# A hybrid decoder block in fp32r: operand tiles moved to other SBUF offsets, three copies moved between ScalarE and VectorE, and one step of the decay sums brought forward

## The reference, cut to what matters

```python
h = rms_norm(x, norm_pre_w)
proj = h @ w_in                                  # 10256 columns
qkv_a, z_a, beta_a, dec_a, qkv_b, z_b, gate_logits = split(proj)   # beta_a, dec_a: 8 columns each
qkv_a = silu(causal_depthwise_conv(qkv_a, conv_w))
beta = sigmoid(beta_a)
g = -exp(dn_a_log) * softplus(dec_a + dn_dt_bias)
oa = gated_delta_rule(qa, ka, va, g, beta)       # uses running sums of g and exp of their differences
ya = rms_norm(oa, dn_onorm_w) * silu(z_a)
ob = causal softmax attention(qb, kb, vb) with a relative-position bias
yb = ob * silu(z_b)
gates = sigmoid(gate_logits + b_gate)
merged = gates[0] * (ya @ w_branch[0]) + gates[1] * (yb @ w_branch[1])
out = x + rms_norm(merged @ w_out, norm_post_w)
```

## Time and profile before

| what | value |
|---|---|
| median of three runs | 364.14 us |
| profiled execution, its own time | 364.33 us |
| its span in the trace | 362.5 us |
| granted TensorE clock | 0.998 of full |
| TensorE busy (matmul) | 352.6 us, 97% |
| VectorE, ScalarE, GpSimd busy | 74%, 61%, 16% |
| DMA, mean rate | 172 GB/s |

### The profile page before, as it was taken

The page is one execution under the profiler, slowest core; times in us unless marked ns, Lnnn a source line. Parts: engine busy times, 40 slices in busy tenths (PEclk is TensorE's granted clock), DMA queues, the critical chain, the costliest instruction groups (busy, mean ns, idle before and its releaser), DMA issues.

```text
span 362.5 us, 7455 instructions
## 1 busy us (share of the span) xinstructions
PE 352.6 (97%) x2755; PEld 337.1 (93%) x2755; DVE 267.5 (74%) x559; ACT 222.3 (61%) x500; POOL 59.5 (16%) x113
## 2 busy tenths in 40 slices
PE   7999999999999999999999999999999999999893
PEld 5889997999999999999999999999999999998682
DVE  2869777488986868979787897878976656576744
ACT  4778895545466576686767677677685645334431
POOL 1533434400052000301103030030301000000011
PEclk9999999999999999999999999999999999999999
DMA  8667848896699484456645564475447557583533
GB/s 264 171 189 190 278 122 229 205 289 174 172 254 213 121 223 123 118 133 169 166 118 146 153 168 118 121 202 143 118 121 199 147 152 196 142 266 116 203 146 116
DMA packets 100305, 62.48 MB, mean 172 GB/s; under 512 B 4676, under 2 KB 95214, under 8 KB 100270
## 3 DMA queue, kind: packets, MB, share of 16 engines
q1 hardware_dynamic: 98014, 58.59, 59.1%
q0 software_dynamic: 1072, 3.04, 2.8%
q10 hardware_dynamic: 1184, 0.39, 0.5%
HBM read 60.41 MB, written 1.59 MB: 171 GB/s over the span
## 4 chain that ended last, share of the span: by engine, by line
PE 88%; DVE 4%; ACT 3%; DMA 1%; issue 1%; POOL 0%; DVEq 0%; SPq 0%; ACTq 0%; POOLq 0%
PE banks L1321 62%; PE banks L1339 6%; PE banks L1534 5%; ACT w_hi L637 3%; DVE w_lo L887 2%; DMA xin<-in_x_dram 1%; PE banks L1419 1%; PE banks L1396 1%; DVE th_E L1169 1%; PE banks L1436 1%; PE banks L1425 1%; PE banks L1306 1%; DVE th_a L1165 1%; PE banks L1238 1%; PE banks L1385 1%
## 5 line engine op out<-in xcount | busy, mean ns | idle before, releaser
L887 DVE TENSOR_TENSOR w_lo<-raw,w_hi 128x1024 fp32r<-128x1024 f32 x102 | 123.9, 1218 | 54.3 <-ACT w_hi L637 51.3
L637 ACT CAST w_hi<-raw 128x1024 fp32r<-128x1024 f32 x103 | 107.2, 1045 | 8.4 <-DMA raw<-in_w_out_dram 3.5
L1321 PE MATMUL banks<-h_hi,w_hi 128*128 128x256 f32 x568 | 82.1, 286 | 0.0
L1321 PE MATMUL banks<-h_lo,w_hi 128*128 128x256 f32 x568 | 78.0, 279 | 0.0
L1321 PE MATMUL banks<-h_hi,w_lo 128*128 128x256 f32 x568 | 77.8, 279 | 0.0
L1321 PEld LDWEIGHTS banks<-h_hi,w_hi 128*128 128x128 f32 x568 | 71.4, 188 | 0.3
L1321 PEld LDWEIGHTS banks<-h_hi,w_lo 128*128 128x128 f32 x568 | 71.2, 188 | 0.0
L1321 PEld LDWEIGHTS banks<-h_lo,w_hi 128*128 128x128 f32 x568 | 71.2, 188 | 0.0
L961 DVE SCALAR_TENSOR_TENSOR acc<-banks,vec,acc 128x255 f32<-128x255 f32 (+2 forms) x72 | 34.5, 479 | 4.3 <-ACT acc L758 2.2
L587 POOL TENSOR_TENSOR so<-so,rnq 128x2 f32<-128x2 f32 x8 | 2.6, 329 | 164.9 <-ACT junk L825 164.9
L758 ACT ACTIVATE acc<-banks,vec 128x256 f32<-128x256 f32 x16 | 7.6, 473 | 19.2 <-PE banks L1321 19.2
(11 more groups left out here) (243 smaller groups left out, 545.5 us busy)
## 6 DMA issues: line engine op xcount, KB each, us to landing
raw<-in_w_in_dram SPq DMA_DIRECT2D x80, 512.0 KB, 5.2
raw<-in_w_branch_dram SPq DMA_DIRECT2D x16, 512.0 KB, 4.9
raw<-in_w_out_dram SPq DMA_DIRECT2D x8, 512.0 KB, 3.7
xin<-in_x_dram SPq DMA_DIRECT2D x2, 512.0 KB, 4.0
th_E<-g_rows POOLq DMA_DIRECT2D x2, 512.0 KB, 7.0
bias<-bias_rows POOLq DMA_DIRECT2D x1, 1024.0 KB, 7.6
raw<-in_x_dram SPq DMA_DIRECT2D x2, 512.0 KB, 5.7
out_dram<-xin SPq DMA_DIRECT2D x4, 256.0 KB, 2.0
```

Source lines behind the costliest of these rows:

```text
L637: nc.scalar.copy(w_hi[:, t % SLOTS, :], raw[:, t % SLOTS, :]).then_inc(s_hi, 1)
L887: v.tensor_tensor(w_lo[:, t % SLOTS, cols], raw[:, t % SLOTS, cols], w_hi[:, t % SLOTS, cols].bitcast(F32), ALU.subtract).then_inc(s_lo, 1)
L1321: last = mm(ps, w, r, start=part == 0 and k == 0, stop=part == 2 and k == KT - 1)
```

## The change

The order of the allocations changes, and three pieces of work move:
- `gt` (768 bytes of a partition), `wbd2` (1024), `ssqk` (64) and `ng` (64) are declared ahead of `raw`: 1920 bytes in all. `h_hi`, `h_lo`, `y_hi` and `y_lo` are declared behind `w_lo`. By the sizes, `raw`, `w_hi`, `w_lo`, `h_hi`, `h_lo`, `y_hi`, `y_lo`, `xin` and `cst` then start at multiples of 2 KB. `acc` and what follows it keep their offset past a multiple of 2 KB (576 for `acc`, `kT_all`, `act`, `bT`).
- The copy to `bd_T` at S = 5 goes from VectorE to ScalarE.
- The copies of the first half of `vtok_all` at S = 33 and 34 go from ScalarE to VectorE.
- VectorE's last step of g (L941 to L947) goes from S = 9 to S = 8, ahead of that step's `split_lo`.

```diff
+        gt = sb("gt", [P, 12, NC, HEADS])
+        wbd2 = sb("wbd2", [P, KT, 4 * HEADS], F32R)
+        ssqk = sb("ssqk", [P, NC, HEADS])
+        ng = sb("ng", [P, NC, HEADS])
         raw = sb("raw", [P, SLOTS, D])
         w_hi = sb("w_hi", [P, SLOTS, D], F32R)
         w_lo = sb("w_lo", [P, SLOTS, D], F32R)
+        h_hi = sb("h_hi", [P, KT, SEQ], F32R)
+        h_lo = sb("h_lo", [P, KT, SEQ], F32R)
+        y_hi = sb("y_hi", [P, 2, HEADS, SEQ], F32R)
+        y_lo = sb("y_lo", [P, 2, HEADS, SEQ], F32R)
         xin = sb("xin", [P, NC, D])
...
-        wbd2 = sb("wbd2", [P, KT, 4 * HEADS], F32R)
...
-        h_hi = sb("h_hi", [P, KT, SEQ], F32R)
-        h_lo = sb("h_lo", [P, KT, SEQ], F32R)
...
-        gt = sb("gt", [P, 12, NC, HEADS])
...
-        ng = sb("ng", [P, NC, HEADS])
...
-        ssqk = sb("ssqk", [P, NC, HEADS])
...
-        y_hi = sb("y_hi", [P, 2, HEADS, SEQ], F32R)
-        y_lo = sb("y_lo", [P, 2, HEADS, SEQ], F32R)
```

On ScalarE:

```diff
-                if S == 7:
+                if S == 5:
+                    sa.wait_ge(s_bd_m, 1)
+                    nc.scalar.copy(bd_T, bA[0:4 * HEADS, 0:SEQ]).then_inc(s_bd_t, 1)
+                elif S == 7:
...
-            def value_front(i):
-                group, c = i // NC, i % NC
+            def value_front(c):
                 if c == 0:
-                    sa.wait_ge(s_vg_p, group + 1)
+                    sa.wait_ge(s_vg_p, 2)
                 else:
-                    sa.wait_ge(s_tile, V_TILES[4 * group + 3] + 1)
-                nc.scalar.copy(vtok_all[:, c, 512 * group:512 * group + 512],
-                               ((bE, bF), (bB, bE))[group][c]).then_inc(s_vtok, 1)
+                    sa.wait_ge(s_tile, V_TILES[7] + 1)
+                nc.scalar.copy(vtok_all[:, c, 512:], (bB, bE)[c]).then_inc(s_vtok, 1)
```

On VectorE (`value_front` is called behind `similarity`, at S = 33 and 34):

```diff
-                if S == 5:
-                    ve.wait_ge(s_bd_m, 1)
-                    v.tensor_copy(bd_T, bA[0:4 * HEADS, 0:SEQ]).then_inc(s_bd_t, 1)
-                elif S == 7:
+                if S == 7:
...
-                elif S == 9:
+                elif S == 8:
                     ve.wait_ge(s_ga, 5)
                     ve.wait_ge(s_gs, 7)
...
+            def value_front(c):
+                if c == 0:
+                    ve.wait_ge(s_vg_p, 1)
+                else:
+                    ve.wait_ge(s_tile, V_TILES[3] + 1)
+                v.tensor_copy(vtok_all[:, c, 0:512], (bE, bF)[c]).then_inc(s_vtok, 1)
```

More of the change, by code:

```diff
@@ L844, in _ @@
                     decay(2 * (S - E0) + 1)
[L845 to L848, removed]
+                done = 3 * V_TILES[7] + 3
+                if S in (done, done + 1):
+                    value_front(S - done)
                 for g in range(HEADS):
@@ L1183, in _ @@
                     similarity(SIM[S])
+                done = 3 * V_TILES[3] + 3
+                if S in (done, done + 1):
+                    value_front(S - done)
                 for g in range(HEADS):
```

## The result

The changed kernel takes 368.75 us (median of four runs, 368.60 to 368.83) beside 364.22 us for the kernel before in the same comparison: ratio 1.0114, 95% interval 1.0088 to 1.0141. Its profiled execution took 368.75 us, with a span of 367.0 us, 4.5 us more than before's 362.5.

The account below looks back on a forecast made before the run. TensorE's own matmul pace was taken to bound most of the kernel, except the loop near the end. Value copies gave -0.22 us and the other three parts 0: 364.14 - 0.22 = 363.9 us, range 355.0 to 366.4.

Parts of the forecast that it names:

- Part 1, value copies: Value copies moved to VectorE end TensorE's wait at L1385 in key head 7; gain 0.20 to 0.25 us.
- Parts 2 and 3: The bd_T copy on ScalarE and the last step of g at S = 8: each taken as 0.
- Part 4, addresses: New start offsets of the tensors leave the matmul pace unchanged: taken as 0, ends -15 us and +2.2 us.
- for no effect: Argument for 0 from addresses: moving operands at different offsets past 2 KB, with stationary offsets differing as much, keep one pace.
- The prediction's own sign of being wrong: The prediction is wrong if the pace of the stream of 384 matmuls, 45.2 us, moves at all.
- The half-sentence *against: Counterpoint to no address effect: no moving operand or weight tile starts at a multiple of 256 bytes, so that grid was untried.
- The rule cited from the Trainium skill: TensorE waits for nobody at SBUF; only VectorE and GpSimd contend, so the address gain is 0.
- The estimate from "DMA: Bandwidth & Descriptors": First load of xin, 4.68 us: a start off a 256-byte boundary costs an extra transaction, estimated 0.28 us.
- The loop near the end: From 311.52 to 336.17 us VectorE and ScalarE bound seven rounds of 3.52 us; faster matmuls win nothing there.
- Rival three: The 22 fast tiles of the heads turn slow, 0.10 us each: +2.2 us, 366.1 us with part 1; chance 0.12.
- Rivals one and two: One: all tiles fast, stream 43.7 us, 356.8 us, chance 0.16. Two: no loss at all, 348.4 us, chance 0.10.
- the last chance, 0.05: Chance given to another wait or a pace slower than now: 0.05.

Follow-up runs that it names:

- the empty one: Block left out but for copying its input; groups of 48 fp32r matmuls with nothing else running: 120.0 ns a matmul at distance 0, 117.8 at 64.
- the 32-byte one: Changed kernel with h and y 32 bytes further than w instead of 0: 364.39 us, ratio 1.0001 to the kernel before.

## Why the prediction was wrong

**Part 1, value copies: right.** The timeline of VectorE with the moves alone (L991 is the new copy, L971 before's L974):

```profile
49.82 1.27 DVE L991 COPY vtok_all<-banks 128x512 f32<-128x512 f32 x2
51.33 1.23 DVE L887 TENSOR_TENSOR w_lo<-raw,w_hi 128x1024 fp32r<-128x1024 f32 x1 [0.23 <-ACT w_hi L637]
...
55.94 0.42 DVE L971 SCALAR_TENSOR_TENSOR kT_all<-tacc,acc 128x256 f32<-128x256 f32 x1
```

The execution is 0.44 us ahead of before's since the load of xin (4.24 us for 4.68 at the same address). The two copies take 1.27 us (predicted 1.36), the next `w_lo` begins at 51.33, 51.77 by before's clock (predicted 51.75), and the last step of key head 7 begins at 55.94, 56.38 by before's clock (57.35 before, 56.6 predicted). L1385's wait for L974 is gone; in the weight load's waits of the changed kernel nothing stands where it stood:

```profile
PEld banks L1278 <- issue: 0.4, 1, 0.4
```

The value stream begins 0.68 us earlier than before, 0.44 of it the load, so the part is worth 0.24 us. The medians give 0.44 (363.70 to 364.14); what the 0.2 beyond come from no run settles, and the ratio's interval, 0.9951 to 1.0000, is wider than that.

**Parts 2 and 3: right at 0.** L1278 keeps its 0.4 us at the issue, and no chain piece before 60 us is shorter or longer with the moves alone but by the wait above.

**Part 4, addresses: the step that failed, at the value 0 taken for it.** The argument *for no effect* was that moving operands at 1984, 704 and 128 all ran at one pace. But it looked at each operand's own start. What counts is the start of one less that of the other, and for h and y before's were the same in this measure: 1984 - 128 = 1856 = 7 x 256 + 64, and 704 - 128 = 576 = 2 x 256 + 64. The third, w at 128 past h at 1984, is 192 modulo 256, and a matmul of 512 columns, so it was no second sample. "Stationary offsets differ as much" was false modulo 256: every slice of `w_hi` and `w_lo` starts 128 past a multiple of 256. What I read as independent offsets was one distance, so its evenness could say nothing about another. The new layout puts the distance at 0, the slowest of the multiples of 16 bytes measured: 120.0 ns for 117.8. The term taken as 0 measured 5.05 us (363.70 to 368.75): in the ledger 0.84 on the long stream and 4.4 on the tiles behind it, with 0.37 won back in the output. The prediction's own sign of being wrong, that the stream's pace moves at all, came true. The half-sentence *against* (no start at a multiple of 256 was ever tried) asked for the wrong grid too: with w and h both at 128 the pace is 120.0 as well.

The rule cited from the Trainium skill, "SBUF — State Buffer", section "Who interferes with whom", gives TensorE two read ports, one for moving data and one for weights, independent, and has it wait on nobody. By it the gain is 0, as taken. The runs disagree as far as TensorE's own two reads go: 113.3 to 123.3 ns by their distance alone. Of other engines it may hold, since the paces of the full kernel and of the empty one agree at distances 0 and 64 to 0.1 ns (120.0 and 117.8). At 128 bytes they did not (120.0 in the long stream, 118.6 by itself), and why stays open.

The estimate from "DMA: Bandwidth & Descriptors", section "How a descriptor splits into AXI transactions", was 0.28 us on the load of xin. No run shows that there: xin took 4.24 us at 128 and 4.27 at 0, and in the other profiles 4.68 at 128, and 4.18 to 4.34 and once 5.20 at 0. For the weight tiles the runs agree with the rule. The changed kernel's page, queue and issue, then that of everything 128 bytes further (packets, MB, share of 16 engines; KB each, us to landing):

```profile
q1 hardware_dynamic: 98014, 58.59, 55.0%
...
raw<-in_w_in_dram SPq DMA_DIRECT2D x80, 512.0 KB, 4.8
```

```profile
q1 hardware_dynamic: 98014, 58.59, 58.6%
...
raw<-in_w_in_dram SPq DMA_DIRECT2D x80, 512.0 KB, 5.3
```

The seven kernels with `raw` at a multiple of 256 bytes (the 32-byte one left out) have 54.9 to 56.6%; the six with it at 128 have 58.6 to 59.4%. The chain of the changed kernel has no wait for a weight tile in its long stretches, so it buys nothing here.

**The loop near the end: right.** Its seven tiles cost nothing by their pace, as the earlier trace rows had it. From the last 72 matmuls before it to the first output matmul the chain takes 339.10 - 302.31 = 36.79 us with the moves alone and 344.62 - 307.69 = 36.93 after; the 72 matmuls (8.65 us for before's 8.50) are the whole difference.

**The rivals.** Rival three (fast tiles lost, 366.1) had the sign and the place, with 2.2 us. Measured on those 22 tiles are 3.1 us: the 2.2 us and another 0.9 since the slow pace under them moved too. But it had no word for the slow tiles, the stream among them, becoming slower still, and that is the larger part of the loss. What it said *against* itself, that the small matmuls ahead keep their offsets, was false: their cst was among the tensors that moved, which the front of this document lists. Rivals one and two named a prize that exists in part: 112 bytes give 43.60 us for the stream, where rival one wanted 43.7; but it comes by distance, not by alignment. The time is above the range's end of 366.4 because the range left out the far slow side: a pace slower than any seen was part of the last chance, 0.05.

## What to carry to other kernels

Before trusting that a pace does not depend on where things lie, list what the cases have in common in differences, not only in absolute values. For a kernel bound by fp32r matmuls of 256 columns, try the moving operand's start 112 bytes past the stationary one's modulo 256, and not the same remainder: here this kernel is 7.5 us faster than the one at 368.75 and 1% faster than the kernel before. Rounding all operand tiles to a common alignment gave the slow pace here. Four bytes more are far worse (122.5 ns at 116), so measure the pace of one continuous stream after every change of the layout: what is allocated between the two operands sets their distance.

## What the runs showed that I had not expected

- TensorE's fp32r pace depends on the distance of its own two operands modulo 256 bytes, by up to 10 ns of 113 (113.3 at 112 bytes, 122.5 at 116, 123.3 at 4), with nothing else running.
- For 512 columns it goes the other way: 226.7 ns at distance 0 and 228.4 to 236.6 elsewhere. The output took 16.61 to 16.91 us in the three kernels with distance 0, and 16.99 to 17.06 in the others.
- Some distances have two steady paces (117.8 and 113.3 at 64 and 192), and what precedes chooses; in the kernel, moving xin, cst and the small tensors behind them by 128 bytes (and h and y 2 KB further from w) took the faster pace away for 1.7 us. Which relation decides was not found.
- A single stationary column takes 113.3 ns at distance 0, where 128 columns take 120.0 and 32 columns 117.8.
